# First mix: order of GpSimd's additions, of taps and head copies, and of mean, centring and squares

## The reference

```
q, k, v, u = split(h @ w_in)                 # 512, 512, 512, 1024 columns
attn = causal softmax attention of 8 heads of rms-normed, rotated q, k
a, g = split(u);  c = a * sigmoid(g)         # gated linear unit, 512 channels
c = causal depthwise convolution of c with 31 taps per channel
c = silu(layer_norm(c) * ln_g + ln_b)        # mean and variance over 512 channels
x = x + concat(attn, c) @ w_out
```

## Time and profile before

| | us |
|---|---|
| median of 3 runs | 1287.52 (1287.06 to 1287.67) |
| the profiled execution, its own time | 1287.17 |
| its span, first to last instruction | 1285.2 |
| TensorE busy | 1275.1 |
| VectorE busy | 838.4 |
| ScalarE busy | 676.2 |
| GpSimd busy | 116.9 |

### The profile page before, as it was taken

The page is one execution under the profiler, slowest core; times in us unless marked ns, Lnnn a source line. Parts: engine busy times, 40 slices in busy tenths (PEclk is TensorE's granted clock), DMA queues, the critical chain, the costliest instruction groups (busy, mean ns, idle before and its releaser), DMA issues.

```text
span 1285.2 us, 18284 instructions
## 1 busy us (share of the span) xinstructions
PE 1275.1 (99%) x7072; PEld 1090.4 (85%) x7072; DVE 838.4 (65%) x1103; ACT 676.2 (53%) x903; POOL 116.9 (9%) x135
## 2 busy tenths in 40 slices
PE   8999999999999999999999999999999999999998
PEld 8988888888888888887888888888888877888886
DVE  7997655565655548898765556655565776675552
ACT  6876554444544435656564444544454665564441
POOL 3860000000000000021000000000002120000000
PEclk9999999999999999999999999999999999999999
DMA  9425765563765553527565555675553755475530
GB/s 290 164 83 187 253 215 196 196 203 120 241 206 183 187 157 115 180 81 249 197 225 184 184 194 162 200 259 196 191 187 127 243 160 165 149 238 184 185 143 33
DMA packets 174350, 234.95 MB, mean 183 GB/s; under 512 B 4351, under 2 KB 154127, under 8 KB 174288
## 3 DMA queue, kind: packets, MB, share of 16 engines
q1 hardware_dynamic: 170368, 223.52, 53.0%
q0 software_dynamic: 3184, 9.37, 2.3%
q10 hardware_dynamic: 736, 1.19, 0.3%
HBM read 233.03 MB, written 1.05 MB: 182 GB/s over the span
## 4 chain that ended last, share of the span: by engine, by line
PE 97%; DVE 2%; ACT 0%; POOL 0%; DMA 0%; issue 0%; DVEq 0%; SPq 0%; ACTq 0%
PE psum L1227 23%; PE psum L1122 15%; PE psum L1123 15%; PE psum L1124 15%; PE psum L1235 12%; PE psum L1248 2%; PE psum L1190 2%; PE psum L1189 2%; PE psum L1188 2%; PE psum L1459 1%; PE psum L1252 1%; PE psum L1507 1%; PE psum L1350 1%; PE psum L1472 1%; PE psum L1149 0%; POOL ws L1012 0%
## 5 line engine op out<-in xcount | busy, mean ns | idle before, releaser
L1894 DVE TENSOR_TENSOR w_lo<-raw,w_hi 128x2048 fp32r<-128x2048 f32 (+1 forms) x200 | 458.6, 2298 | 83.8 <-ACT w_hi L474 82.4
L474 ACT ACTIVATE w_hi<-raw 128x2048 fp32r<-128x2048 f32 (+1 forms) x212 | 403.4, 1907 | 32.6 <-PE psum L1124 13.6
L1227 PE MATMUL psum<-t_both,w_hi 128*128 128x512 f32 x1280 | 304.8, 390 | 0.0
L1227 PEld LDWEIGHTS psum<-t_both,w_hi 128*128 128x128 f32 x1280 | 237.4, 188 | 47.5
L1122 PE MATMUL psum<-w_hi,f_hi 128*128 128x512 f32 x488 | 193.4, 396 | 0.0
L1124 PE MATMUL psum<-w_hi,f_lo 128*128 128x512 f32 x488 | 190.6, 391 | 0.0
L1123 PE MATMUL psum<-w_lo,f_hi 128*128 128x512 f32 x488 | 190.6, 391 | 0.0
L1122 PE MATMUL psum<-w_hi,t_both 128*128 128x512 f32 (+2 forms) x464 | 165.6, 357 | 0.0
L1124 PE MATMUL psum<-w_hi,t_both 128*128 128x512 f32 (+2 forms) x464 | 162.4, 350 | 0.0
L1123 PE MATMUL psum<-w_lo,t_both 128*128 128x512 f32 (+2 forms) x464 | 162.3, 350 | 0.0
L1235 PEld LDWEIGHTS psum<-t_both,w_lo 128*128 128x128 f32 x1280 | 158.9, 192 | 3.1
(11 more groups left out here) (218 smaller groups left out, 1289.3 us busy)
## 6 DMA issues: line engine op xcount, KB each, us to landing
raw<-in_ffn_wg SPq DMA_DIRECT2D x44, 1024.0 KB, 5.6
raw<-in_ffn_wu SPq DMA_DIRECT2D x44, 1024.0 KB, 5.4
raw<-in_ffn_wd SPq DMA_DIRECT2D x44, 1024.0 KB, 5.0
raw<-in_even_w_in SPq DMA_DIRECT2D x12, 1024.0 KB, 5.2
raw<-in_odd_w_in SPq DMA_DIRECT2D x12, 1024.0 KB, 5.4
raw<-in_w_gate SPq DMA_DIRECT2D x11, 1024.0 KB, 5.6
raw<-in_w_up SPq DMA_DIRECT2D x11, 1024.0 KB, 5.4
raw<-in_w_down SPq DMA_DIRECT2D x11, 1024.0 KB, 5.0
```

The lines of the kernel that those rows point to most:

```text
L474: nc.scalar.activation(w_hi[:, n % SLOTS, 0:w], raw[:, n % RAWS, 0:w], ACT.Copy).then_inc(hi_done, 1)
L1227: mm = nc.tensor.matmul(bank[b + c][:, :], wh[:, k, c * P:(c + 1) * P], t_both[:, k, :, :].rearrange("p a s -> p (a s)"), start=k == 0 and ...
L1894: nc.vector.tensor_tensor(w_lo[:, n % SLOTS, 0:w], raw[:, n % RAWS, 0:w], w_hi[:, n % SLOTS, 0:w].bitcast(F32), ALU.subtract).then_inc(lo_ ...
```

## The change

- GpSimd: additions 6, 7 and 11 wait for the low parts of units 5, 6 and 7 as well. The root of unit 4 moves from behind addition 10 to behind addition 8; that of unit 5 stays behind addition 13.
- VectorE: 13 taps instead of 11 come before unit 5's low part (3 of them before unit 3's), with fewer behind; the order of the two groups among the taps changes.
- ScalarE: two products stand before the exponentials of heads 4 and 5 instead of three, the third comes behind `keep_sums`; `keep_pt(L, 5)` moves ahead of a product and of the exponentials of head 6.
- The mean's matmuls take group 1 first and wait for each group's input alone. Centring and squares go in two halves; the sums of squares wait for each half, and go to bank 5 instead of 4.

```diff
+        ADD_BEHIND = {6: 6, 7: 7, 11: 8}
-        DVE_TAPS = [(tap, 0) for tap in range(11)]
-        for n in (3, 2, 5, 3, 2, 2, 9, 5, 3, 5, 8):
-            for i in range(n):
-                ct = 0 if i % 2 else 2
-                DVE_TAPS.append((sum(c == ct for _, c in DVE_TAPS), ct))
+        DVE_TAPS = []
+        for ct in map(int, "0000000000000" "202" "20" "20202" "202" "20" "20" "20202022" "0202022" "20" "20202" "022022"):
+            DVE_TAPS.append((sum(c == ct for _, c in DVE_TAPS), ct))
@@ ScalarE, mix_first
                 keep_pt(L, 3)
-                taps(3)
+                taps(2)
                 exps(L, 4)
                 exps(L, 5)
                 keep_sums(1, V["inv"][0])
+                taps(1)
                 keep_pt(L, 4)
                 taps(1)
                 group_hi(0, 6, scaled=True)
+                keep_pt(L, 5)
                 taps(1)
                 exps(L, 6)
-                keep_pt(L, 5)
                 exps(L, 7)
...
-                act.wait_ge(cen_ok, 1)
-                nc.scalar.activation(V["sq"], V["acc"], ACT.Square).then_inc(sq4_ok, 1)
-                act.wait_ge(sq4_ok, 1)
+                for g in range(2):
+                    act.wait_ge(cen_ok, g + 1)
+                    cts = slice(2 * g, 2 * g + 2)
+                    nc.scalar.activation(V["sq"][:, cts, :], V["acc"][:, cts, :], ACT.Square).then_inc(sq4_ok, 1)
+                act.wait_ge(sq4_ok, 2)
@@ GpSimd, add(n)
                             pool.wait_ge(tap_made, tap + 1)
+                            if tap in ADD_BEHIND:
+                                pool.wait_ge(lo_done, ADD_BEHIND[tap])
...
                     build(2)
-                    add(10)
+                    add(8)
                     root(0)
-                    add(3)
+                    add(5)
                     root(1)
@@ TensorE, mix_first
-                pe.wait_ge(conv_ok, 2)
-                pe.wait_ge(side_ok, 1)
-                for ct in range(4):
-                    mm = nc.tensor.matmul(bank[4][:, 0:S], mean_w[:, :], V["acc"][:, ct, :], start=ct == 0, stop=ct == 3)
+                for ct in (1, 0, 2, 3):
+                    if ct == 1:
+                        pe.wait_ge(tap_added, TAPS - 1)
+                    elif ct == 0:
+                        pe.wait_ge(conv_ok, 2)
+                    elif ct == 2:
+                        pe.wait_ge(side_ok, 1)
+                    mm = nc.tensor.matmul(bank[4][:, 0:S], mean_w[:, :], V["acc"][:, ct, :], start=ct == 1, stop=ct == 3)
                 mm.then_inc(mean_ok, 1)
                 rows(0, 1)
-                pe.wait_ge(sq4_ok, 1)
                 for t in range(T):
                     for ct in range(4):
-                        mm = nc.tensor.matmul(bank[4][:, S + t:S + t + 1], V["sq"][:, ct, t * P:(t + 1) * P], mean_w[:, 0:1],
+                        if t == 0 and ct % 2 == 0:
+                            pe.wait_ge(sq4_ok, ct // 2 + 1)
+                        mm = nc.tensor.matmul(bank[5][:, S + t:S + t + 1], V["sq"][:, ct, t * P:(t + 1) * P], mean_w[:, 0:1],
@@ VectorE, mix_first
                 glu(1)
+                taps(3)
                 split_to(4)
-                taps(2)
+                taps(1)
                 split_to(5)
                 taps(9)
...
                 split_to(11)
-                taps(9)
+                taps(8)
                 rooted_maxima(4)
                 rooted_maxima(5)
-                taps(5)
+                taps(7)
                 group_scale(L, 4, 6, V["inv"][0])
-                taps(3)
+                taps(2)
                 rooted_maxima(6)
                 rooted_maxima(7)
                 group_lo(0, 6)
                 taps(5)
                 group_sums(L, 4)
-                taps(8)
+                taps(6)
...
-                nc.vector.tensor_tensor(V["acc"], V["acc"], bank[4][:, 0:S].unsqueeze(1).broadcast_to([P, 4, S]), ALU.subtract)\
-                    .then_inc(cen_ok, 1)
+                for g in range(2):
+                    cts = slice(2 * g, 2 * g + 2)
+                    nc.vector.tensor_tensor(V["acc"][:, cts, :], V["acc"][:, cts, :], bank[4][:, 0:S].unsqueeze(1).broadcast_to([P, 2, S]), ALU.subtract)\
+                        .then_inc(cen_ok, 1)
```

More of the change, by code:

```diff
@@ L2320, in mix_first @@
                 dve.wait_ge(var_ok, 1)
-                nc.vector.tensor_scalar(st[:, 10:12], bank[4][:, S:S + T], EPS, None, ALU.add).then_inc(ms_ready, 1)
+                nc.vector.tensor_scalar(st[:, 10:12], bank[5][:, S:S + T], EPS, None, ALU.add).then_inc(ms_ready, 1)
                 nx(rstd_ready, 5)
                 dve.wait_ge(spread_ok, 1)
-                dve.wait_ge(cen_ok, 1)
+                dve.wait_ge(cen_ok, 2)
                 for g in range(2):
```

## The result

The changed kernel takes 1288.88 us (1288.35 to 1289.91, 22 runs) against 1287.13 before (1285.39 to 1288.68, 22 runs): ratio 1.0015, 95% interval [1.0009, 1.0021]. It is 1.75 us slower; the forecast was 2.25 us. The profiled execution took 1289.72, with a span of 1287.9. It is the third slowest of the 22, and 2.55 us above the profiled execution of the kernel before (1287.17).

The account below looks back on a forecast made before the run. TensorE was taken as the bound, so only its waits and clock count: 3.0 - 0.35 - 0.4 = +2.25 us on 1287.17 gives 1289.4, as a median 1289.8; range 1285.6 to 1292.0.

Parts of the forecast that it names:

- The bound: TensorE carries 97% of the chain; a change elsewhere counts only by the TensorE waits it removes or makes.
- Part 1: GpSimd's three waits, with root and taps: lags make TensorE wait, 3.0 us lost; bounds nothing to 4.6.
- steps a to c: Lag carried through VectorE, GpSimd and ScalarE from unit 5's low part to unit 5's squares, 4.6 us late at 51.75.
- Step a: VectorE makes 13 taps before unit 5's low part, which starts at 36.3; 0.2 us added for additions 1 and 2.
- step c: GpSimd's root of unit 4 stands ahead of additions 9 and 10; squares of unit 5 start at 51.75, 4.6 us late.
- Step d: Unit 5's third rotary product frees bank 1 for unit 7 at 54.55; TensorE asks at 53.1 and loses 1.45 us.
- Step e: Unit 8's low part, behind late additions and unit 6's squares, ends at 62.9; TensorE loses 1.2 us more.
- Step f: VectorE and ScalarE 3.9 us late, TensorE 2.7; unit 6's turn takes 0.3 more; later inputs come early enough.
- The collisions: VectorE low parts and GpSimd additions exclude each other, the second stands; avoiding them gives VectorE 2.0 us, -2.0 if it bounds.
- Part 2: Late order on ScalarE: the copied head comes ahead of head 6's exponentials, removing TensorE's wait before L1507, -0.35 us.
- Part 3: Mean by groups, centring and squares in halves: shortens TensorE's wait before the one-column matmuls, -0.4 us; bounds -0.2 and -0.5.
- The clock: Half-clock stretch behind the one-column matmuls: assumed to fall again, 0 us; bounds 0 and -1.7; new waits could add +1.7.

Follow-up runs that it names:

- e4: The changed kernel with GpSimd's root of unit 4 back behind addition 10; 1288.00 us, ratio 1.0009 to the kernel before.
- e10: e3 plus GpSimd's root of unit 4 ahead of additions 9 and 10; 1286.18 us, ratio 0.9998 to the kernel before.
- e1: The changed kernel without the three extra waits of GpSimd; 1286.64 us, ratio 1.0001 to the kernel before.
- e2: The kernel before plus the three GpSimd waits, nothing else; 1288.86 us, ratio 1.0013.
- e11: e3 plus all three GpSimd waits, taps and root as before; 1286.97 us, ratio 1.0002 to the kernel before.
- e7: The kernel before plus mean by groups, centring and squares in halves, nothing else; 1285.40 us, ratio 0.9990.
- e3: The kernel before plus the late parts alone (Part 2 and Part 3 without VectorE's taps); 1285.34 us, ratio 0.9990.
- e12: e4 with unit 8's low part moved ahead of the sum of unit 6's squares on VectorE; 1289.95 us, ratio 1.0025 to the kernel before.
- e6: e3 plus the first two waits, additions 6 and 7 behind the low parts of units 5 and 6; 1286.17 us, ratio 0.9996 to the kernel before.
- e8: The kernel before plus the moved copy of the fifth head and one moved product, nothing else; 1286.17 us, ratio 0.9996.

## Why the prediction was right

- **The bound** was right: TensorE's waits and the clock explain thirteen times within 0.7 us.
- **Part 1, steps a to c.** The order came out as carried forward, 0.6 us late from the start: unit 5's low part at 36.87 (forecast 36.3), squares of unit 4 at 44.47 (43.85), of unit 5 at 52.34 (51.75). Step a had put in 0.2 for the collisions of units 3 and 4; their low parts took 2.46 and 2.86 us instead of 2.29 and 2.28, 0.75 in all. The low parts got their 0.4 and 0.5 us back, and VectorE spent them idle, 2.81 us against 2.7. What step c's root costs shows in e4 (2.1 us of the lag of unit 5's squares) and e10 (0.84 us of time for the root alone).
- **Step d** was right: bank 1 free at 55.42 (54.55), a wait of 1.76 us (1.45). Its twin was overlooked: unit 4's third rotary product ends at 47.23, and TensorE, which began unit 6 at 46.94 before, waits for bank 0.
- **Step e** was right on VectorE, and its wait hides behind the clock. Unit 8's low part ended at 63.94 (62.9), but in this trace nobody waited for it: TensorE ran at half clock from 57.0 to 60.4 and came only at 64.25. Without the fall TensorE would have stood at 63.94, only 0.3 us sooner. The fall took the place of the forecast wait and came on top of it by those 0.3 us; the three executions without it, as slow as the rest, say the same. e4, e1 and e2, where the clock did not fall there, show the forecast wait: 1.31, 0.99 and 1.30 us.
- **Step f:** right for what follows; no further wait in the first mix. The 0.3 us for the turn of unit 6 came as 0.2 (4.0 us late before it, 4.2 at it).
- **The collisions.** That of an addition and a low part the one that comes second stands is confirmed where the waits avoid the collision: the low parts take 2.29 us again. The reading that this makes VectorE's order the bound, -2.0, is refuted by e2. Its other side, an addition pushed behind a whole low part, is what e2 and e11 cost.
- **Part 2** right: the wait before L1507 went. **Part 3** right in sign; e7 gives 1.5 us instead of 0.4, since the fall of the clock went with the wait. In the kept traces parts 2 and 3 are worth what was forecast: the lag of 4.2 us at the turn of unit 6 is 3.6 at the one-column matmuls.
- **The clock** is the term that I had wrong. I took 0, because the only stretch of this kind fell. The old fall went in all kernels with the halves, and it was worth 1.0 us, not the 1.7 that half of 3.4 us gives, since TensorE is held by VectorE again just behind it. A new fall came behind the 1.76 us wait, but mostly in the place of a wait. The late parts alone, without waits, root and taps, are a change of -1.7 us (e3); the whole change without the three waits is one of -0.4 (e1).
- **The sum** was near by luck. In the two kept traces waits and new fall put TensorE 4.2 us back at the turn of unit 6, where 3.0 were forecast; the late parts gave back 0.6 of the forecast 0.75; the old fall gave back 1.0, where 0 was forecast. Two errors of 1.2 and 1.0 us with opposite signs leave 2.6 where the sum says 2.25. The medians, which also hold executions of the kernel before without a fall, differ by 1.75. The sign, and the path that made it, were not luck.

## What to carry to other kernels

A wait that avoids a collision pays only if the engine that it frees sets the end; here it moved VectorE's loss from slow instructions into idle time, and made three engines late one after another. Add up all lags that reach one and the same needed input before comparing them with its slack: each of the waits, the root and the taps passed or nearly passed alone (0.15, 0.8, 0.8 and 0 us), together they cost 3.5 (1288.88 against e3's 1285.34), the new fall included. And before idle time is filled, look at what the filler collides with: e12's low part moved its collision from a root that has time to one that has none, and cost 1.9 us. A stretch at half clock costs half its length only if nothing else bounds the engine there and just behind it.

## What the runs showed of the hardware

- A root of eight columns on GpSimd takes 1.68 us alone, and 3.72 to 3.83 us when VectorE's subtraction with two SBUF inputs lies over it: 3.72 when the subtraction began 0.07 us before it (kernel before), 3.83 when it began 0.03 us after it (e12, where the subtraction took 2.29 us, as alone). So for this root it is not the one that comes second that stands, as far as the starts in the trace tell. A tiny operation loses as much as a large one: 2.1 us here, 1.9 for the addition at 35.74.
- In the kept traces the clock fell to 1.2 GHz for 3.4 us behind TensorE waits of 1.76 us (the change) and 2.82 us (e12), and not behind those of 1.31 (e4), 1.30 (e2), 1.01 (e6) and 0.99 (e1). It varies from one execution to the next: 3 of 22 of the change have a mean granted clock of 1.000.
- Behind sixteen one-column matmuls with about 0.2 us of idleness ahead of them it fell in the kept traces of the kernel before and of e2, and not in that of e8 (0.16). Without that idleness it fell in no trace, and none of 99 executions of nine such kernels reads 0.997, which 24 of 97 of the kernel before do.
- Such a stretch of 3.4 us at half clock cost 1.0 us where VectorE held TensorE just behind it (e8 against the kernel before), and some 0.3 us where a low part was about to be late anyway (the change).
